# Norm tiles with the feature weight and the spread root in one DVE instruction, the shift on ACT, and both blocks of the first job by tile

## The chip, the cores and the metric

One core of one Trainium2 chip. The metric is device time in microseconds of one launch: 2413.69 us is the median of three runs of the kernel before (2411.8 to 2418.44).

## The reference, cut to what matters

A two-layer block over 512 latent tokens and 256 context tokens of width 1024. Layer 0 mixes with an SSD scan and a long convolution, layer 1 with windowed attention; each has a SwiGLU feed-forward. Ahead of each of these four projections every token vector is normed, weighted by feature and shifted by feature:

```
def rmsnorm(t, g):
    y = t * rsqrt(mean(t * t, axis=-1) + 1e-6)
    return y * g

h_l = rmsnorm(x, norm1_g[layer]) * (1.0 + mod_l[1]) + mod_l[0]      # latent tokens
h_c = rmsnorm(ctx, norm1_g[layer]) * (1.0 + mod_c[1]) + mod_c[0]    # context tokens
p = h @ w_in                                   # layer 0; layer 1: h @ w_qkv
...
h_l = rmsnorm(x, norm2_g[layer]) * (1.0 + mod_l[4]) + mod_l[3]      # before the feed-forward
gu = h_l @ ffn_w_in[layer]
```

So a normed element is x * root(token) * gain(feature, segment) + shift(feature, segment). The two segments are the latent and the context tokens.

## The kernel before

The activations lie with features on the partitions: a tensor is 8 tiles (`KT`) of 128 features by 768 tokens, and `SEGS` are its columns 0 to 511 (latent) and 512 to 767 (context). Layer 1's queries and its feed-forward use the latent columns alone.

Every product is made of three TensorE passes on rounded parts: a high part (rounded to fp32r) and a low part (the rest) for both weights and activations; high x high, high x low weight, low x high weight (L487, L488, L492). The weights' high part is a DVE copy (`split_high`, L1587) into `WH`, which has a single place for each of the two blocks of a job. The low part is a POOL subtraction (`low`, L2013), written over the weights. So the next job's block b can be split only when this job's block b is multiplied (`next_high` waits for `blocks_done`). Weights come in jobs of two 512 KB halves, into 3 slots, issued by SP (L431) when the job three places earlier is multiplied. In the first stage (`uv`) two of each three jobs are small ada jobs, so there the next large job's load is issued when the present one is multiplied.

A norm goes as follows. TensorE sums squares, ACT takes the root (L1178), DVE its reciprocal, and TensorE spreads it into PSUM as `NP` (L565). Then DVE, ACT, POOL and TensorE work tile by tile on 8 tiles: DVE makes the normed tile in `norm` with a multiplication of x by `NP` (L1576) and, after waiting for itself, one `tensor_scalar` per segment with gain and shift (L1578); ACT copies it into its high part (`high_parts`, L1184); POOL subtracts for the low part (`low_parts`, L2026). TensorE's first job after the norm (`two_blocks` with `by_tile`) waits per tile for the high part and then for the low part. It does so in block 0 alone: block 0 takes all 8 tiles, then block 1 takes the 8 tiles again, with no wait.

There are four such places: the `uv` stage (trace 178 to 217 us), layer 0's feed-forward (1104 to 1142 us), the q/k/v stage (1691 to 1728 us; 768 columns are normed, of which its first jobs multiply 512) and layer 1's feed-forward (2024 to 2043 us, 512 columns). In the q/k/v stage POOL issues the rope table's and the mask's loads (L2180, L2181) behind its last low part, and DVE waits for the rope table before it splits any weights of that stage. The final norm (L1573) has no such job behind it.

The key lines before:

```
TT(HN[:, k, lo:hi], X[:, k, lo:hi], NP[:, lo:hi], ALU.mult)              # L1576, DVE
TS(HN[:, k, a:b], HN[:, k, a:b], GA[...], MOD[...], ALU.mult, ALU.add)   # L1578, DVE, per segment
run(high[:, k, lo:hi], HN[:, k, lo:hi], ACT.Copy)                        # L1184, ACT
TT(HNL[:, k, lo:hi], HN[:, k, lo:hi], high[:, k, lo:hi], ALU.subtract)   # L2026, POOL
```

## Time and profile before

| | us |
|---|---|
| median of three runs | 2413.69 (2411.8 to 2418.44) |
| the profiled execution | 2418.78, of which 2417.0 is the span of its trace |
| TensorE busy | 2217.1 |
| DVE, POOL, ACT busy | 960.0, 856.9, 413.7 |
| mean granted TensorE clock | 0.933 |

The page gives busy time by engine, a picture of the span in 40 slices, and groups of instructions by line. The timeline gives single instructions: start, length, engine, line, what is written from what, and in brackets how long the engine was idle before it and who released it. TensorE's granted clock is told as a share: 1.00 is 2.4 GHz and 0.50 is 1.2 GHz. Several matmuls are in flight at once, so the distance between two starts is what one costs.

### The profile page before, as it was taken

The page shows a single profiled execution, that of the slowest core. Times are in us where ns is not written, and L with a number is a line of the kernel's source. Part 1 is how long each engine was busy: PE and PEld are TensorE (multiplying, and loading weights), DVE is VectorE, ACT ScalarE, POOL GpSimd, SP SyncE. Part 2 cuts the span into 40 slices and gives each one's busy share as a digit, 9 for nine tenths or more (in the row PEclk, how much of TensorE's full clock was granted, in tenths as well). Part 3 has the DMA queues.
Part 4 walks back from the last instruction along what each step waited for, and adds up shares of the span by engine and source line. Part 5 has one row for each costly group of instructions (what it writes and reads, how often), then busy time and mean ns, then how long its engine had stood idle before and what let it go on. Part 6 is the DMA issues. An engine that isn't in the chain of part 4 may idle for free. (4 is left out here: it accounts for less than half of the span.)

```text
span 2417.0 us, 30280 instructions
## 1 busy us (share of the span) xinstructions
PE 2217.1 (92%) x11978; PEld 1734.4 (72%) x11978; DVE 960.0 (40%) x1284; ACT 413.7 (17%) x769; POOL 856.9 (35%) x460
## 2 busy tenths in 40 slices
PE   7959998899998996997999999998787998999997
PEld 2436865688887774885888888887475666888886
DVE  3555354321234767335122112133525655322334
ACT  1211111001244553001000000000103631100110
POOL 0264353512223756323222332222421124444442
PEclk8777998999998997997999999999788998999998
DMA  8312432333311001110111221112110002223222
GB/s 302 135 52 96 152 111 101 107 113 126 102 44 53 1 2 43 56 67 26 61 61 48 74 71 61 53 60 70 61 45 18 1 28 69 95 78 112 91 82 73
DMA packets 50750, 181.52 MB, mean 75 GB/s; under 512 B 5815, under 2 KB 6071, under 8 KB 49688
## 3 DMA queue, kind: packets, MB, share of 16 engines
q1 hardware_dynamic: 48288, 163.60, 20.2%
q10 hardware_dynamic: 1848, 13.52, 1.5%
q0 software_dynamic: 512, 2.95, 0.3%
q8 instruction: 75, 1.23, 0.2%
q14 instruction: 27, 0.22, 0.0%
HBM read 177.95 MB, written 2.10 MB: 74 GB/s over the span
## 5 line engine op out<-in xcount | busy, mean ns | idle before, releaser
L2013 POOL TENSOR_TENSOR weights_lo<-weights,weights_hi 128x1024 fp32r<-128x1024 f32 (+1 forms) x232 | 514.4, 2218 | 1042.8 <-DVE weights_hi L1587 1042.8
L492 PE MATMUL psum<-normed_lo,weights_hi 128*128 128x512 f32 x1856 | 550.9, 360 | 12.0 <-POOL normed_lo L2026 11.9
L1587 DVE CAST weights_hi<-weights 128x1024 fp32r<-128x1024 f32 (+1 forms) x232 | 163.9, 707 | 921.1 <-PE psum L492 786.4
L487 PE MATMUL psum<-normed_hi,weights_hi 128*128 128x512 f32 (+1 forms) x1152 | 425.2, 369 | 16.1 <-ACT normed_hi L1184 16.1
L488 PE MATMUL psum<-normed_hi,weights_lo 128*128 128x512 f32 (+1 forms) x1152 | 404.8, 365 | 0.0
L492 PEld LDWEIGHTS psum<-normed_lo,weights_hi 128*128 128x128 f32 x1856 | 306.0, 193 | 43.7 <-POOL normed_lo L2026 26.3
L487 PEld LDWEIGHTS psum<-normed_hi,weights_hi 128*128 128x128 f32 x1152 | 221.6, 192 | 74.4 <-ACT normed_hi L1184 15.2
L487 PE MATMUL psum<-normed_first_hi,weights_hi 128*128 128x512 f32 x704 | 248.5, 353 | 16.1 <-POOL weights_lo L2013 9.3
L488 PEld LDWEIGHTS psum<-normed_hi,weights_lo 128*128 128x128 f32 x1152 | 222.7, 193 | 38.3 <-issue 1.5
L488 PE MATMUL psum<-normed_first_hi,weights_lo 128*128 128x512 f32 x704 | 226.7, 343 | 0.0
L487 PE MATMUL psum<-hidden_hi,weights_hi 128*128 128x512 f32 (+1 forms) x528 | 189.1, 358 | 0.0
L488 PE MATMUL psum<-hidden_hi,weights_lo 128*128 128x512 f32 (+1 forms) x528 | 178.9, 354 | 0.0
L487 PEld LDWEIGHTS psum<-normed_first_hi,weights_hi 128*128 128x128 f32 x704 | 135.8, 193 | 57.3 <-issue 10.8
L492 PE MATMUL psum<-hidden_lo,weights_hi 128*128 128x512 f32 (+1 forms) x528 | 160.4, 358 | 0.0
L488 PEld LDWEIGHTS psum<-normed_first_hi,weights_lo 128*128 128x128 f32 x704 | 136.3, 194 | 17.6 <-issue 1.2
L487 PEld LDWEIGHTS psum<-hidden_hi,weights_hi 128*128 128x128 f32 x528 | 99.1, 188 | 23.5
L488 PEld LDWEIGHTS psum<-hidden_hi,weights_lo 128*128 128x128 f32 x528 | 99.3, 188 | 15.0
L487 PE MATMUL psum<-mixed_hi,weights_hi 128*128 128x512 f32 (+1 forms) x256 | 90.5, 354 | 14.2 <-ACT mixed_hi L1373 8.0
L1618 DVE SCALAR_TENSOR_TENSOR temps<-psum,vectors,temps 128x511 f32<-128x511 f32 x112 | 63.8, 612 | 98.6 <-ACT temps L1198 97.6
L492 PEld LDWEIGHTS psum<-hidden_lo,weights_hi 128*128 128x128 f32 x528 | 87.1, 188 | 8.9
L1389 ACT ACTIVATE temps<-psum 128x768 f32<-128x768 f32 (+1 forms) x44 | 31.1, 707 | 355.7 <-PE psum L492 355.7
L1393 ACT ACTIVATE hidden_hi<-temps 128x768 f32 (+3 forms) x44 | 32.5, 740 | 342.9 <-DVE temps L1872 342.9
(281 smaller groups left out, 3015.1 us busy)
## 6 DMA issues: line engine op xcount, KB each, us to landing
weights<-in_wall SPq DMA_DIRECT2D x264, 512.0 KB, 4.0
weights<-in_wall SPq DMA_DIRECT2D x32, 384.0 KB, 3.2
weights<-in_wall SPq DMA_DIRECT2D x32, 320.0 KB, 3.0
residual<-in_xT ACTq DMA_DIRECT2D x2, 3072.0 KB, 10.4
phase<-in_tab ACTq DMA_DIRECT2D x3, 1280.0 KB, 7.0
out_T<-normed SPq DMA_DIRECT2D x2, 1024.0 KB, 4.3
normed<-in_window ACTq DMA_DIRECT2D x1, 1536.0 KB, 16.7
normed<-in_window POOLq DMA_DIRECT2D x1, 1536.0 KB, 7.7
```

The costliest lines, as they stand in the source:

```text
L487: mm(acc[:, lo:hi], WH[:, b, k, :], high[:, lo:hi], start=st, stop=False)
L488: mm(acc[:, lo:hi], WL[:, s, HALF * b + k, :], high[:, lo:hi], start=False, stop=False)
L492: ins = mm(acc[:, lo:hi], WH[:, b, k, :], low[:, lo:hi], start=False, stop=en)
L1389: run(T[:, 0, lo:hi], pair(0)[:, lo:hi], ACT.Silu).then_inc(pair_free[0], 1)
L1393: run(at_row(HIDH, r)[:, lo:hi], T[:, 1, lo:hi], ACT.Copy).then_inc(hid_hi, 1)
L1587: dve.tensor_copy(WH[:, b, 0:n, :], W[:, s, HALF * b:HALF * b + n, :]).then_inc(w_hi, 1)
L1618: ins = STT(t[:, a:e], p[:, a + shift:e + shift], w, t[:, a:e], ALU.mult, ALU.add)
L2013: TT(WL[:, s, at, :], W[:, s, at, :], WH[:, b, 0:width(gs[0], b), :].bitcast(f32), ALU.subtract).then_inc(w_lo, 1)
```

## The change

In `norm`, the two steps of DVE become one `scalar_tensor_tensor` per segment, (x * gain) * spread root, which reads x from SBUF and `NP` from PSUM. The shift moves to ACT: `high_parts` first runs one Identity activation per segment in place on the normed tile, with the shift as a per-partition bias, waits for itself, and then makes the high copy as before. A new function `both_by_tile` serves the first job of each of the four places: both blocks' weights and PSUM pairs are waited for at the start, then tiles 0 to 5 are multiplied for both blocks as they come, then tiles 6 and 7 for block 0, then tiles 6 and 7 for block 1.

```diff
--- before.py
+++ after.py
@@ -492,11 +492,42 @@
                         ins = mm(acc[:, lo:hi], WH[:, b, k, :], low[:, lo:hi], start=False, stop=en)
                 ins.then_inc(blocks_done, 1)
 
+            def both_by_tile(gs, i, rhs, segs, by_tile, after=None, last=True, together=6):
+
+
+                s = gs[0] % SLOTS
+                accs = []
+                for b in range(2):
+                    half_ready(gs, i, b)
+                    accs.append(pair(pair_ready(gs, i, b)))
+                order = [(k, (0, 1)) for k in range(together)] + [(k, (b,)) for b in range(2) for k in range(together, KT)]
+                for k, blocks in order:
+                    if blocks[0] == 0:
+                        by_tile[0](k)
+                    high, low = rhs(k)
+                    for b in blocks:
+                        for lo, hi in segs:
+                            mm(accs[b][:, lo:hi], WH[:, b, k, :], high[:, lo:hi], start=k == 0, stop=False)
+                            mm(accs[b][:, lo:hi], WL[:, s, HALF * b + k, :], high[:, lo:hi], start=False, stop=False)
+                    if blocks[0] == 0:
+                        by_tile[1](k)
+                    for b in blocks:
+                        for lo, hi in segs:
+                            ins = mm(accs[b][:, lo:hi], WH[:, b, k, :], low[:, lo:hi], start=False,
+                                     stop=last and k == KT - 1)
+                    if k == KT - 1:
+                        ins.then_inc(blocks_done, 1)
+                    if after:
+                        after(k, blocks)
+
             def two_blocks(gs, i, rhs, segs=SEGS, between=None, by_tile=None):
+                if by_tile:
+                    both_by_tile(gs, i, rhs, segs, by_tile)
+                    return
                 for b in range(2):
                     half_ready(gs, i, b)
                     u = pair_ready(gs, i, b)
-                    tiles(gs, pair(u), b, KT, rhs, segs, True, True, by_tile if b == 0 else None)
+                    tiles(gs, pair(u), b, KT, rhs, segs, True, True)
                     if b == 0 and between:
                         between()
 
@@ -1177,16 +1208,19 @@
                 n = 2 * segs[-1][1] // P
                 run(RS[0][:, 0:n], NS[:, 0:n], ACT.Sqrt, scale=1.0 / D, bias=vec("eps", 0)).then_inc(n_sqrt, 1)
 
-            def high_parts(muls, segs=SEGS, high=HNH):
+            def high_parts(muls, layer, shift, segs=SEGS, high=HNH):
                 lo, hi = segs[0][0], segs[-1][1]
                 for k in range(KT):
                     act.wait_ge(n_mul, muls + k + 1)
+                    for j, (a, b) in enumerate(segs):
+                        ins = run(HN[:, k, a:b], HN[:, k, a:b], Id, bias=MOD[:, layer, 8 * shift + k, j:j + 1])
+                    ch.link(ins)
                     run(high[:, k, lo:hi], HN[:, k, lo:hi], ACT.Copy).then_inc(hn_hi, 1)
 
 
             act.wait_ge(n_summed, 1)
             root()
-            high_parts(0, high=HNH0)
+            high_parts(0, 0, 0, high=HNH0)
 
             def conv_first(gs, i, b, wname, bname, blk, dst, wait=None):
 
@@ -1376,7 +1410,7 @@
                 sqrt_table()
                 act.wait_ge(n_summed, n + 1)
                 root(segs)
-                high_parts(KT * (n + 1), segs)
+                high_parts(KT * (n + 1), layer, 3, segs)
                 lo, hi = segs[0][0], segs[-1][1]
                 for half in range(2):
                     name = f"up{layer}{half}"
@@ -1399,7 +1433,7 @@
             sqrt_table()
             act.wait_ge(n_summed, 3)
             root()
-            high_parts(3 * KT)
+            high_parts(3 * KT, 1, 0)
 
             for n in range(5):
                 g = AT["qkv"] + n
@@ -1560,7 +1594,7 @@
                         ins = TT(even, even, odd, ALU.subtract)
                     ins.then_inc(kd_ev, 1)
 
-            def norm(n, which=None, layer=0, shift=0, segs=SEGS, last=False):
+            def norm(n, which=None, segs=SEGS, last=False):
 
                 lo, hi = segs[0][0], segs[-1][1]
                 dve.wait_ge(n_sqrt, n + 1)
@@ -1573,10 +1607,9 @@
                         STT(HN[:, k, lo:hi], X[:, k, lo:hi], vec("fin", k), NP[:, lo:hi], ALU.mult, ALU.mult) \
                             .then_inc(fin_ready, 1)
                         continue
-                    ch.link(TT(HN[:, k, lo:hi], X[:, k, lo:hi], NP[:, lo:hi], ALU.mult))
                     for j, (a, b) in enumerate(segs):
-                        ins = TS(HN[:, k, a:b], HN[:, k, a:b], GA[:, which, k, j:j + 1],
-                                 MOD[:, layer, 8 * shift + k, j:j + 1], ALU.mult, ALU.add)
+                        ins = STT(HN[:, k, a:b], X[:, k, a:b], GA[:, which, k, j:j + 1], NP[:, a:b],
+                                  ALU.mult, ALU.mult)
                     ins.then_inc(n_mul, 1)
 
 
@@ -1605,7 +1638,7 @@
             ins.then_inc(mods_a, 1)
             dve.wait_ge(mods_a, 1)
             ch.link(gains(0, 0, 1, "n1"))
-            norm(0, 0, 0, 0)
+            norm(0, 0)
 
             def conv(gs, i, b, wname, n, blk, count, dst=None):
 
@@ -1858,7 +1891,7 @@
                     dve.memset(MARK[:, 0:1], 0.0).then_inc(sums_ready, 1)
 
             def feed_forward(layer, n, segs):
-                norm(n + 1, 2 * layer + 1, layer, 3, segs)
+                norm(n + 1, 2 * layer + 1, segs)
                 lo, hi = segs[0][0], segs[-1][1]
                 for half in range(2):
                     name = f"{layer}{half}"
@@ -1882,7 +1915,7 @@
             dve.wait_ge(x_in, 32)
             res("out0", 0, 2, SEGS)
             feed_forward(0, 1, SEGS)
-            norm(3, 2, 1, 0)
+            norm(3, 2)
 
 
             dve.wait_ge(rope_in, 16)
```

## Rows read from the trace of the kernel before

**Rows 1.** The page's first part: busy time of TensorE, share, instructions.
```profile
PE 2217.1 (92%) x11978; PEld 1734.4 (72%) x11978; DVE 960.0 (40%) x1284; ACT 413.7 (17%) x769; POOL 856.9 (35%) x460
```

**Rows 2.** Timeline, first normed tiles: start us, length us, engine, line, operation, [idle before].
```profile
178.39 0.95 DVE L1576 TENSOR_TENSOR normed<-residual,psum 128x768 f32<-128x768 f32 x1 [3.02 <-PE psum L565]
...
181.15 2.48 DVE L1578 TENSOR_SCALAR normed<-normed,gains,mods 128x512 f32<-128x512 f32 x2
...
181.20 1.82 POOL L2026 TENSOR_TENSOR normed_lo<-normed,normed_first_hi 128x768 fp32r<-128x768 f32 x1 [4.01 <-ACT normed_first_hi L1184]
...
181.27 0.47 PE L487 MATMUL psum<-normed_first_hi,weights_hi 128*128 128x512 f32 x1 [2.92 <-ACT normed_first_hi L1184]
```

**Rows 3.** Line L1844 (one PSUM, one SBUF input): count, minimum/median/maximum ns.
```profile
L1844 DVE SCALAR_TENSOR_TENSOR residual<-psum,mods,residual x72: 468/744/751, 973.3 to 2400.7; 128x512 f32 x30, 128x512 f32<-128x512 f32 x18, 128x256 f32 x18, 128x256 f32<-128x256 f32 x6
```

**Rows 4.** Groups of ACT by shape, SBUF to SBUF: busy us, mean ns.
```profile
L1184 ACT ACTIVATE normed_hi<-normed 128x768 fp32r<-128x768 f32 x16 | 13.5, 843 | 45.8 <-DVE normed L1578 45.8
...
L1393 ACT ACTIVATE hidden_hi<-temps 128x512 f32 x18 | 11.4, 632 | 114.6 <-DVE temps L1872 114.6
...
L1274 ACT ACTIVATE phase<-phase,vectors 128x768 f32<-128x768 f32 x8 | 7.5, 931 | 0.0
```

**Rows 5.** Timeline of ACT, eight copies with no wait between them.
```profile
903.51 5.98 ACT L1362 ACTIVATE mixed_hi<-phase 128x768 fp32r<-128x768 f32 x8
```

**Rows 6.** Timeline from block 1 of the first job to the next job's start.
```profile
207.51 0.63 PE L487 MATMUL psum<-normed_first_hi,weights_hi 128*128 128x512 f32 x1
...
207.75 0.99 ACT L1198 ACTIVATE temps<-psum,vectors 128x768 f32<-128x768 f32 x1 [2.99 <-PE psum L492]
...
209.43 0.56 PE L487 MATMUL psum<-normed_first_hi,weights_hi 128*128 128x512 f32 x1
...
212.14 0.69 DVE L1587 CAST weights_hi<-weights 128x1024 fp32r<-128x1024 f32 x1 [1.06 <-DMA weights<-in_wall]
...
212.92 2.40 POOL L2013 TENSOR_TENSOR weights_lo<-weights,weights_hi 128x1024 fp32r<-128x1024 f32 x1 [6.27 <-DVE weights_hi L1587]
...
217.01 1.92 PE L523 MATMUL psum<-weights,phase 128*32 128x512 f32 x16
...
218.87 0.50 PE L487 MATMUL psum<-normed_first_hi,weights_hi 128*128 128x512 f32 x1
```

**Rows 7.** The same of layer 0's feed-forward: block 1 starts, refill, block 1 ends.
```profile
1133.15 0.63 PE L487 MATMUL psum<-normed_hi,weights_hi 128*128 128x512 f32 x1
...
1134.17 2.40 POOL L2013 TENSOR_TENSOR weights_lo<-weights,weights_hi 128x1024 fp32r<-128x1024 f32 x1 [1.88 <-DVE weights_hi L1587]
...
1142.52 0.69 DVE L1587 CAST weights_hi<-weights 128x1024 fp32r<-128x1024 f32 x1 [8.43 <-PE psum L492]
```

**Rows 8.** The same of the q/k/v stage, with the rope table's load.
```profile
1694.37 0.77 PE L487 MATMUL psum<-normed_hi,weights_hi 128*128 128x512 f32 x1 [2.92 <-ACT normed_hi L1184]
...
1719.67 0.58 POOL L2180 DMA_DIRECT2D phase<-in_rope  x1
...
1723.61 0.69 DVE L1587 CAST weights_hi<-weights 128x1024 fp32r<-128x1024 f32 x1 [6.66 <-DMA phase<-in_rope]
...
1728.39 0.69 DVE L1587 CAST weights_hi<-weights 128x1024 fp32r<-128x1024 f32 x1 [4.08 <-PE psum L492]
```

**Rows 9.** The same of layer 1's feed-forward, 512 columns.
```profile
2025.92 0.77 PE L487 MATMUL psum<-normed_hi,weights_hi 128*128 128x512 f32 x1 [2.11 <-ACT normed_hi L1184]
...
2037.61 0.40 PE L487 MATMUL psum<-normed_hi,weights_hi 128*128 128x512 f32 x1
...
2043.38 0.69 DVE L1587 CAST weights_hi<-weights 128x1024 fp32r<-128x1024 f32 x1 [4.88 <-PE psum L492]
```

**Rows 10.** Stretches: length, TensorE busy us (count), granted clock, DMA share, GB/s.
```profile
182.40:206.70 24.30, 18.59 (x42) 0.50 0.08 20
...
2025.90:2032.40 6.50, 6.11 (x13) 0.50 0.00 0
...
1750.20:1756.00 5.80, 3.67 (x7) 0.71 0.28 90
```

## The prediction

> **What bounds the kernel now.** I read the page's first part, then the timeline at the four places that the change touches. TensorE is busy 92% of the span [rows 1], so the time falls only where TensorE waits or runs at its low clock, and outside the four places nothing is touched. At the first place the reader is to see a relay. DVE's multiplication starts at 178.39, TensorE's first matmul at 181.27 and block 1 of the same job at 207.51 [rows 2, 6]. Block 0 thus takes 26.24 us for 8 tiles, 3.28 us a tile, while its matmuls cost far less: at the full clock block 1 shows 7 tiles in 7.58 us (209.43 to 217.01) [rows 6], the first of them partly slow, and layer 1's feed-forward shows 8 tiles of 512 columns in 5.53 us (2037.61 to the cast at 2043.38, less the 0.24 us from matmul to cast seen at 207.51 and 207.75) [rows 6, 9]: 0.69 for 512 columns, so 1.04 for 768. I take 1.05 and 0.70. Nor is DVE's own work 3.28 us. Its `tensor_scalar` pair starts at 181.15 and needs 2.48 us, and POOL's subtraction starts at 181.20 and ends at 183.02 [rows 2]: the first of the pair waits for POOL. So in the normed tiles DVE bounds, held up by POOL, and TensorE waits at 0.50 of its clock, which is its 1.2 GHz level [rows 10].
>
> **Part 1: DVE.** Removed per tile: a 768-column multiplication (0.95 us), a wait on itself, and the pair of 2.48 us [rows 2]. Added: two `scalar_tensor_tensor` with one input in PSUM. The residual additions have this form: median 744 and at most 751 ns at 512 columns, 468 at 256, over 72 that ran beside POOL's work as well as without it, so POOL never held one up [rows 3]. I take 0.74 + 0.47 = 1.2 us a tile. DVE no longer waits for anybody and is done with 8 tiles after some 10 us.
>
> The Trainium skill (SBUF — State Buffer, Who interferes with whom) says that DVE and GpSimd share a pair of ports that one instruction holds for its whole length, and that a DVE instruction with at most one SBUF input, outside the two-port modes, does not contend. It would make the `tensor_scalar` the culprit and the new form free. The trace agrees: 2.48 us beside POOL's 1.82 us [rows 2], 751 ns at most for the other form [rows 3].
>
> **Part 2: ACT.** Before, one copy: 843 ns at 768 columns, 632 at 512 [rows 4]; that is 0.21 us per 256 columns, so some 421 ns at 256. Added per tile: two Identity activations with a vector operand, and a wait of ACT for itself. An activation with one vector operand took 931 against 843 ns, 88 more [rows 4]. So 0.72 + 0.51 us, less the overlap of neighbours: eight copies took 5.98 us, not 6.74, 0.11 each [rows 5]. ACT's wait for itself is not shown; the nearest row is a handover between engines, DVE's cast (end 212.83) to POOL (212.92), 0.09 us [rows 6]. Inside one engine I take 0.05, with 0.2 as the dear end; below 0 it cannot go, since it only orders two instructions. Period of ACT: 0.72 + 0.51 - 0.11 + 0.05 + 0.84 - 0.08 = **1.93 us** for 768 columns, and 0.72 + 0.05 + 0.63 - 0.08 = 1.32 us for 512; without overlaps and with the dear wait 2.3 and 1.55. POOL needs 1.82 and some 0.07 for the handover, which hides behind ACT. The first tile comes at 178.39 + 1.15 (DVE) + 1.12 + 0.05 + 0.84 (ACT) + 0.14 (two handovers) = 181.69 instead of 181.27 [rows 2]: **0.42 us** later.
>
> **Part 3: both blocks by tile.** Per tile TensorE now has 2 x 1.05 = 2.1 us of work against ACT's 1.93, so it bounds and hides ACT and POOL. Sixteen tile-blocks cost 16.8 us at the full clock. To this comes 0.5 us in the first tile: the high passes of both blocks last 1.4 us, the low part comes after 1.9. And the clock is low at first: in the relay it was 0.50 throughout [rows 10], and once TensorE no longer waited (207.51) it reached full pace by 209.43, where a tile then took 1.08 instead of 1.92 us [rows 6]. I take 5 us at the low level, which costs 2.5 us; the ends are 1.9 us as at 207.51 (costs 1.0) and 7 us (costs 3.5), since from 2025.90 to 2032.40 TensorE was busy 6.11 of 6.50 us and still at 0.50 [rows 10].
>
> What is late next is the refill of the weights. The next job's block 0 can be split only when block 0 is done. Before, block 1 hid this: 8 tiles. Now only tiles 6 and 7 of block 1 do, 2.1 us.
>
> *Place 1 (uv).* Before: block 1 begins at 207.51, ACT reads block 0 at 207.75, the next weights must still be loaded (the cast waits for their DMA until 212.14), and POOL's low part ends at 215.32 [rows 6]. The refill takes 7.9 us. After: TensorE starts at 181.27 + 0.42 = 181.7, ends block 1 at 181.7 + 16.8 + 0.5 + 2.5 = 201.5 and block 0 at 199.4. The next large job starts at 199.4 + 7.9 = 207.3; the ada job between them covers only 1.9 of it (217.01 to 218.87) [rows 6], so TensorE stands some 3.9 us. Before, it started at 218.87: 11.6 us earlier. A wait is followed by low clock: 1750.20 to 1756.00 holds a wait of some 2 us (3.67 busy of 5.80) and a mean clock of 0.71 [rows 10], so 0.58 x 5.80 = 3.4 us at the low level, which cost 1.7. I charge 1.8 us (0 to 2.5). **Gain 9.8** (7.8 to 12.9). The SP queue holds the loads behind `blocks_done` in the same order as before, and POOL's product and DVE's convolution stand ahead of block 1's refill, which has the next block 0 (8.4 us) as cover.
>
> *Place 2 (layer 0's feed-forward).* The loads are here long since. The refill is 1133.15 to POOL's end at 1136.57, 3.5 us with the handover [rows 7]. The relay was as long as at place 1, so it began at 1106.9; now 1107.3. End of block 1 at 1107.3 + 19.8 = 1127.1, of block 0 at 1125.0, next job at 1128.5, a wait of 1.4 us. Before: 1142.52 - 0.24 = 1142.3. 13.8 us, less 0.8 for the clock (0 to 1.8): **gain 13.0** (11.1 to 15.2).
>
> *Place 3 (q/k/v).* Norm of 768 columns, matmuls of 512: 1.4 us a tile, so ACT bounds with 1.93. Start 1694.37 + 0.42 = 1694.8, last high part 13.5 later, last low part at 1710.2. Then POOL issues the rope load, and DVE's next cast waits for it, 3.94 us from issue (1719.67 to 1723.61) [rows 8]: 1714.2. Cast and low part take 3.3: TensorE's next job at 1717.5, though it was done with the first at 1711.9. Before: 1728.39 - 0.24 = 1728.15. 10.6 us, less 1.8 for the clock: **gain 8.8** (7.4 to 10.6; a later tile of ACT, up to 0.37 us each, would take 2.6 more).
>
> *Place 4 (layer 1's feed-forward).* The relay is short here: blocks 0 and 1 together take 2025.92 to 2043.1 [rows 9]. After: 2026.1 + 16 x 0.70 + 0.3 + 2.5 = 2040.1, block 0 at 2038.7, refill 3.5, next job at 2042.2. 0.9 us, less 1.2 for the clock: **-0.3** (-1.9 to 2.3).
>
> **The sum.** 9.8 + 13.0 + 8.8 - 0.3 = 31.3 us (24.4 to 41.0, all bounds one way). The profiled execution took 2418.78 us, its span 2417.0; the median is 2413.69. Its span would become 2385.7 and its time 2387.5. That execution lies 5.1 us above the median, spread over 2417 us, so the gain carries over whole: 2413.69 - 31.3 = **2382.4 us**.
>
> **The rivals.** *A, the clock stays low in the joint jobs.* The condition is that small gaps between the groups of two accumulations keep the clock at 0.50. A tile-block is then 1.92 us (207.51 to 209.43) [rows 6], 1.28 for 512 columns. Place 1: block 1 ends at 212.4, block 0 at 208.6, next job 216.5, 2.4 less 1.0 for the clock; place 2: 1138.0, 4.3; place 3 stays with the rope load at 8.8; place 4: 2026.1 + 20.5 = 2046.6, 3.5 lost. Together 11.0: **2402.7 us**. For it: at 0.50 TensorE was busy 18.59 of 24.30 us and did not rise [rows 10]. Against it: here the work never runs out. Chance 8%.
>
> The Trainium skill (TensorE: Matmul & The Clock Gate, A second HAM failure mode: psum-queue depth-cycling) tells of a kernel that cycled through PSUM banks, stood briefly between its groups and so lost its clock again and again. That is rival A, as the joint job changes its PSUM pair twice a tile; by the forecast that rule does not bite. No row here shows two accumulations in turn.
>
> *B, the new DVE form waits for POOL after all.* A tile then takes 1.82 + 1.2 + 0.05 = 3.07 us, 2.1 at 512 columns. Place 1's next job starts at 213.5 (3.6 gained with the clock), place 2's at 1134.7 (6.8), place 3's at 1725.4 (1.0), place 4 loses 3.5: 7.9, **2405.8 us**. 751 ns at most speaks against it [rows 3]. Chance 4%.
>
> *C, slower: ACT becomes the relay's bound.* The mechanism is what ACT must do between Identity and Copy, a reload of its function tables above all; its place is the 32 normed tiles. With x us more per tile, the next jobs start at 205.5, 1126.7, 1717.5 and 2040.5, each plus 8x. Against the starts before, that gives 13.4 + 15.6 + 10.6 + 2.6 - 32x, less some 5.6 for the clock, so it decides from x = 1.1 us. At x = 2.5 it costs 43 us: **2457 us**. Against it: at 207.75 ACT ran an Identity right behind the root and the copies with nothing in front but its wait for TensorE [rows 6]. Chance 3%.
>
> *D, part of the gain is given back later*, where place 1's head start meets the next loads, since each large job there waits for a load that is issued when the one before ends. The next block's refill of 7.9 us has 8.4 + 1.9 us of cover, a margin of 2.4 us only. If all of place 1 is lost: **2392 us**. Chance 6%.
>
> *E, no low clock anywhere*, neither at the start nor behind the new waits: all upper bounds, some 41 us, **2373 us**. Chance 7%.
>
> **How the numbers follow.** The forecast, 2382.4 with 2373 to 2389 from the bounds, has 72%; A 8, B 4, C 3, D 6, E 7%. The range for 8 in 10 goes to D, E and A, as the clock is the least certain term: 2371 to 2403. A measurement of this kernel tells 0.3%, 7.2 us, from no change. Faster by more: 0.94. Within it: 0.03 (B or C in part). Slower by more: 0.03 (C).
>
> **What would show it.** In the trace after: DVE's new line at 0.74 and 0.47 us also beside POOL's subtraction; ACT's period at 1.9 us with no table load inside; first-job matmuls gapless from the second tile on, block 1's end near 201.5, 1127, 1712 and 2040; then waits of some 3.9, 1.4, 5.5 and 2 us, ended by POOL's low weights, with a low clock behind the longer ones. Wrong would be: tiles of 1.9 us in TensorE to the end (A), DVE idle or stretched beside POOL (B), ACT above 3 us a tile (C), and later `uv` jobs that wait more than before (D).

## The result and the profile after

The changed kernel took 2382.35 us (median of four runs, 2380.05 to 2386.81), the kernel before 2414.68 us beside it (2411.8 to 2418.44): a ratio of 0.9859, 95% interval 0.9842 to 0.9875. The profiled execution of after took 2386.81 us with a span of 2385.0; forecast were 2387.5 and 2385.7.

The page's first part of the kernel after, columns as in [rows 1]:

```profile
PE 2192.0 (92%) x11978; PEld 1731.1 (73%) x11978; DVE 905.8 (38%) x1252; ACT 443.5 (19%) x825; POOL 856.4 (36%) x460
```

TensorE runs the same 11978 matmuls and is busy 25.1 us less. At the low clock a matmul of 512 columns is busy 0.63 us (207.51 in [rows 6]) and at the full clock 0.39 (188.16 below), so this is relay time that is gone. DVE loses 54.2 us, ACT gains 29.8, POOL is as before.

The timeline of the kernel after at place 1, to be read against [rows 2, 6]:

```profile
179.03 8.49 DVE L1611 SCALAR_TENSOR_TENSOR normed<-residual,gains,psum 128x512 f32<-128x512 f32 x16 [3.02 <-PE psum L596]
180.20 1.12 ACT L1216 ACTIVATE normed<-normed,mods 128x512 f32<-128x512 f32 x2 [4.53 <-DVE normed L1611]
...
182.28 15.09 POOL L2059 TENSOR_TENSOR normed_lo<-normed,normed_first_hi 128x768 fp32r<-128x768 f32 x8 [4.46 <-ACT normed_first_hi L1218]
182.34 0.47 PE L510 MATMUL psum<-normed_first_hi,weights_hi 128*128 128x512 f32 x1 [3.35 <-ACT normed_first_hi L1218]
...
188.16 0.39 PE L510 MATMUL psum<-normed_first_hi,weights_hi 128*128 128x512 f32 x1
...
190.26 0.39 PE L510 MATMUL psum<-normed_first_hi,weights_hi 128*128 128x512 f32 x1
...
198.68 0.39 PE L510 MATMUL psum<-normed_first_hi,weights_hi 128*128 128x512 f32 x1
198.88 0.99 ACT L1232 ACTIVATE temps<-psum,vectors 128x768 f32<-128x768 f32 x1 [3.44 <-PE psum L516]
...
202.90 0.69 DVE L1620 CAST weights_hi<-weights 128x1024 fp32r<-128x1024 f32 x1 [0.68 <-PE psum L554]
203.67 2.34 POOL L2046 TENSOR_TENSOR weights_lo<-weights,weights_hi 128x1024 fp32r<-128x1024 f32 x1 [6.31 <-DVE weights_hi L1620]
206.07 0.50 PE L487 MATMUL psum<-normed_first_hi,weights_hi 128*128 128x512 f32 x1 [3.28 <-POOL weights_lo L2046]
```

The reader is to see four things. DVE makes all 16 segments in 8.49 us without a stop. POOL's eight subtractions start 1.89 us apart (15.09 us in all), the distance at which ACT makes the tiles without a pause, so the relay runs at ACT's pace; POOL is close behind, its subtractions last 1.84 to 1.86 us each. TensorE goes from tile to tile in 2.10 us (188.16 to 190.26), both blocks together (from here on the joint job), and has block 0 done at 198.68. Then it stands 3.28 us, until POOL has the low part of the next weights: the relay has made room for a new wait.

The waits of TensorE at the four places of the kernel after (line, released by: us in total, times, longest), by windows 150 to 260, 1075 to 1150, 1645 to 1730 and 1975 to 2060 us:

```profile
PE psum L487 <- POOL weights_lo L2046: 3.3, 1, 3.3
...
PE psum L487 <- POOL weights_lo L2046: 1.2, 1, 1.2
...
PE psum L487 <- POOL weights_lo L2046: 5.7, 1, 5.7
PE psum L516 <- POOL normed_lo L2059: 2.0, 4, 0.9
...
PE psum L487 <- POOL weights_lo L2046: 1.9, 1, 1.9
```

And what TensorE's clock did (stretch: length, busy us of PE, PEld, DVE, ACT, POOL, clock, DMA share, GB/s): from the first matmul of place 1 for 3.76 us, the rest of the joint job, and 3.5 us behind the new waits of places 1 to 4.

```profile
182.34:186.10 3.76, 3.76 (x13) 3.23 (x14) 3.76 (x8) 3.70 (x7) 3.66 (x3) 0.56 0.00 0
186.10:198.50 12.40, 12.40 (x72) 10.85 (x71) 1.42 (x3) 9.18 (x15) 11.08 (x6) 1.00 0.24 82
...
206.07:209.57 3.50, 3.50 (x13) 3.03 (x14) 1.84 (x1) 0.00 (x0) 2.87 (x2) 0.59 0.97 303
1117.49:1120.99 3.50, 3.50 (x20) 3.07 (x21) 2.59 (x3) 0.85 (x1) 2.41 (x1) 1.00 0.42 147
1692.73:1696.23 3.50, 3.50 (x8) 2.81 (x9) 0.00 (x0) 0.00 (x0) 2.28 (x1) 0.50 0.06 23
2008.92:2012.42 3.50, 3.50 (x8) 2.80 (x9) 2.72 (x3) 0.63 (x1) 2.37 (x1) 0.51 0.41 142
```

To place the gain I cut both traces at DVE's reciprocal that heads each norm, which stands at 175.14, 1100.75, 1688.23, 2021.47 and (final norm) 2404.5 us before, and at 175.78, 1091.21, 1663.51, 1988.38 and 2372.51 after. A stretch from one to the next holds one place and what follows it. "At the next job" is the gain in the time from the reciprocal to the first matmul of the next large job.

| place | at the next job: forecast | measured | given back after it: forecast | measured | gain: forecast | measured |
|---|---|---|---|---|---|---|
| 1, uv | 11.6 | 13.4 | 1.8 | 3.3 | 9.8 | 10.2 |
| 2, layer 0's feed-forward | 13.8 | 15.3 | 0.8 | 0.1 | 13.0 | 15.2 |
| 3, q/k/v | 10.6 | 10.7 | 1.8 | 2.3 | 8.8 | 8.4 |
| 4, layer 1's feed-forward | 0.9 | 1.1 | 1.2 | 2.2 | -0.3 | -1.1 |
| sum | 36.9 | 40.5 | 5.6 | 7.9 | 31.3 | 32.6 |

The first reciprocal came 0.64 us later after than before; that leaves 32.0, the difference of the spans.

### The profile page after: what moved, and what is told of

Read it like the earlier page. It is cut to its first block, busy times and chain, and to the rows that moved or that the text cites. A ratio compares the mean times of both kernels' runs of the same rounds, so it can differ in the third digit from the quotient of the medians.

```text
span 2385.0 us, 30305 instructions
## 1 busy us (share of the span) xinstructions
PE 2192.0 (92%) x11978; PEld 1731.1 (73%) x11978; DVE 905.8 (38%) x1252; ACT 443.5 (19%) x825; POOL 856.4 (36%) x460
## 4 chain that ended last, share of the span: by engine, by line
PE 83%; DVE 6%; POOL 6%; DMA 2%; ACT 1%; issue 1%; ACTq 0%; DVEq 0%; SPq 0%
PE psum L487 20%; PE psum L492 20%; PE psum L488 20%; PE psum L1068 2%; PE psum L1056 2%; PE psum L1085 2%; PE psum L554 1%; POOL weights_lo L2046 1%; PE psum L708 1%; DMA weights<-in_wall 1%; PE psum L893 1%; PE psum L918 1%; PE psum L676 1%; DVE normed L1793 1%; PE psum L638 1%
## 5 line engine op out<-in xcount | busy, mean ns | idle before, releaser
L492 PE MATMUL psum<-normed_lo,weights_hi 128*128 128x512 f32 x1760 | 511.9, 354 | 0.0
L487 PE MATMUL psum<-normed_hi,weights_hi 128*128 128x512 f32 x1088 | 394.5, 363 | 8.8 <-POOL weights_lo L2046 8.8
L488 PE MATMUL psum<-normed_hi,weights_lo 128*128 128x512 f32 x1088 | 376.8, 361 | 0.0
L492 PEld LDWEIGHTS psum<-normed_lo,weights_hi 128*128 128x128 f32 x1760 | 287.7, 191 | 16.9
L487 PEld LDWEIGHTS psum<-normed_hi,weights_hi 128*128 128x128 f32 x1088 | 206.6, 190 | 57.7 <-POOL weights_lo L2046 6.4
L487 PE MATMUL psum<-normed_first_hi,weights_hi 128*128 128x512 f32 (+1 forms) x672 | 235.6, 351 | 11.8 <-POOL weights_lo L2046 11.3
L488 PEld LDWEIGHTS psum<-normed_hi,weights_lo 128*128 128x128 f32 x1088 | 207.7, 191 | 35.3 <-issue 1.0
L488 PE MATMUL psum<-normed_first_hi,weights_lo 128*128 128x512 f32 (+1 forms) x672 | 215.8, 342 | 0.0
L487 PEld LDWEIGHTS psum<-normed_first_hi,weights_hi 128*128 128x128 f32 x672 | 129.3, 192 | 48.1 <-POOL weights_lo L2046 13.2
L488 PEld LDWEIGHTS psum<-normed_first_hi,weights_lo 128*128 128x128 f32 x672 | 129.6, 193 | 16.6 <-issue 1.2
L487 PE MATMUL psum<-mixed_hi,weights_hi 128*128 128x512 f32 (+1 forms) x256 | 91.5, 357 | 14.2 <-ACT mixed_hi L1407 8.0
L1427 ACT ACTIVATE hidden_hi<-temps 128x768 f32 (+3 forms) x44 | 32.6, 740 | 334.2 <-DVE temps L1905 334.2
## 6 DMA issues: line engine op xcount, KB each, us to landing
residual<-in_xT ACTq DMA_DIRECT2D x2, 3072.0 KB, 10.6
```

What stands on the lines that cost most here:

```text
L487: mm(acc[:, lo:hi], WH[:, b, k, :], high[:, lo:hi], start=st, stop=False)
L488: mm(acc[:, lo:hi], WL[:, s, HALF * b + k, :], high[:, lo:hi], start=False, stop=False)
L492: ins = mm(acc[:, lo:hi], WH[:, b, k, :], low[:, lo:hi], start=False, stop=en)
L1427: run(at_row(HIDH, r)[:, lo:hi], T[:, 1, lo:hi], ACT.Copy).then_inc(hid_hi, 1)
```

## The experiments

Theory 1 is the account of the prediction: the old pace of 3.3 us a tile came from DVE being held up by POOL, the new form ends that, and the joint multiplication trades an earlier end of block 1 for a wait on the refill. Its rivals are told in each expectation. All runs of a batch stand beside the kernel before on the same chip (medians there 2416.01, 2416.41 and 2417.25 us), and ratios are to it.

**Each half of the change alone.** First the new norm without the joint job:

```diff
-                if by_tile:
-                    both_by_tile(gs, i, rhs, segs, by_tile)
-                    return
...
-                    tiles(gs, pair(u), b, KT, rhs, segs, True, True)
+                    tiles(gs, pair(u), b, KT, rhs, segs, True, True, by_tile if b == 0 else None)
```

> The changed kernel with both blocks of the first job taken one after the other again, block 0 by tile, block 1 behind it; the norm's new split between DVE and ACT stays. Theory 1 (the relay's pace is what paid, and the joint job gives most of its own gain back as a wait for the weights' refill): block 0 then ends with the last low part, near 197.5 us at place 1, block 1 hides the refill. Next jobs some 9.8 us (place 1), 9.5 (place 2), 10.7 (place 3) earlier and 0.9 later (place 4) than in the kernel before: 2414 - 29 = 2385 us, within 3 us of the full change, with no wait for low weights behind the first jobs. Theory 2 (the joint job is worth what it takes from block 1, 6.3 us at each 768-column place and more of the gain with it): 2400 us or more.

Measured: 2383.56 us, ratio 0.9866 (0.9852 to 0.988). Then the joint job with the old norm:

```diff
-                        ins = STT(HN[:, k, a:b], X[:, k, a:b], GA[:, which, k, j:j + 1], NP[:, a:b],
-                                  ALU.mult, ALU.mult)
+                    ch.link(TT(HN[:, k, lo:hi], X[:, k, lo:hi], NP[:, lo:hi], ALU.mult))
+                        ins = TS(HN[:, k, a:b], HN[:, k, a:b], GA[:, which, k, j:j + 1],
+                                 MOD[:, layer, 8 * shift + k, j:j + 1], ALU.mult, ALU.add)
```

> The kernel before with the joint multiplication alone; DVE's norm in three instructions with gain and shift, ACT's copy only. Theory 1: the relay still comes at 3.37 us a tile and bounds; the joint job ends some 7 us sooner at places 1 and 2 but the refill then stands open, 7.4 and 3.5 us behind block 0. Gains 2, 5, -0.5 and -0.5: 2414 - 6 = 2408 us. Theory 2 (the joint job carries the gain): 2395 us or less.

Measured: 2410.04 us, ratio 0.9971 (0.9962 to 0.9979). In the same batch the changed kernel itself ran once more:

> The changed kernel itself, as the measure for the other three on the same chip: 2382 us, 31 to 33 us below the kernel before, by either theory.

Measured: 2378.84 us, ratio 0.9851 (0.9832 to 0.9869). So the new norm alone brings 32.5 of the 37.2 us of this batch, the joint job alone 6.0. On top of the new norm the joint job adds 4.7 us by the medians, but the two intervals overlap, so that is not shown to be different from none. A single profile can't decide it either: up to the first norm's reciprocal all kernels of this study run the same code, and yet it stands between 169.93 us (two tiles together) and 177.15 (shift left out). The stretches say where it would be: 576.40 us with the norm alone against 571.33 with both, at place 2, and 914.09 against 913.69 at place 1. Place 1 shows why. Timeline of the kernel with the norm alone, from block 1's first matmul to the next large job:

```profile
195.70 0.39 PE L487 MATMUL psum<-normed_first_hi,weights_hi 128*128 128x512 f32 x1
...
200.47 0.69 DVE L1617 CAST weights_hi<-weights 128x1024 fp32r<-128x1024 f32 x1 [1.22 <-DMA weights<-in_wall]
...
201.24 2.41 POOL L2043 TENSOR_TENSOR weights_lo<-weights,weights_hi 128x1024 fp32r<-128x1024 f32 x1 [6.05 <-DVE weights_hi L1617]
...
206.02 0.50 PE L487 MATMUL psum<-normed_first_hi,weights_hi 128*128 128x512 f32 x1
```

Block 0 is done at 195.7, the refill ends at 203.65 under block 1's eight tiles, and the next job starts at 206.02 with no wait. The joint job takes this cover away and pays with the 3.3 us above and a low clock behind them.

In the kernel with the old norm and the joint job DVE's old pair is still there, and so is its pace:

```profile
182.68 2.51 DVE L1609 TENSOR_SCALAR normed<-normed,gains,mods 128x512 f32<-128x512 f32 x2
...
186.09 2.50 DVE L1609 TENSOR_SCALAR normed<-normed,gains,mods 128x512 f32<-128x512 f32 x2
```

A tile takes 3.41 us (182.68 to 186.09), and TensorE waits for ACT's high part tile after tile.

**How many tiles together.** The number of tiles multiplied for both blocks goes from 6 to 4, then to 2. With fewer, block 0 ends earlier and more of block 1 covers the refill.

```diff
-            def both_by_tile(gs, i, rhs, segs, by_tile, after=None, last=True, together=6):
+            def both_by_tile(gs, i, rhs, segs, by_tile, after=None, last=True, together=4):
```

> The changed kernel with tiles 0 to 3 for both blocks together and tiles 4 to 7 for each block alone (6 and 2 in the changed kernel). Block 0 then ends as soon as the last low part allows, about 1 us sooner than with 6, and block 1's tail of four tiles covers 4.2 instead of 2.1 us of the refill. Theory 1 (the refill behind block 0 is the new bound, so the time follows block 0's end, not block 1's): 1 us less at places 1, 2 and 4 and a shorter wait with less low clock: 2 to 4 us below the full change. Theory 3 (only block 1's end counts): no change.

Measured: 2373.62 us, ratio 0.9827 (0.9814 to 0.984).

> Tiles 0 and 1 for both blocks, tiles 2 to 7 for each block alone. Theory 1: block 0 cannot end sooner than with 4 (it waits for the last low part), while block 1's tail is now 6.3 us, longer than the 3.5 us refill of places 2 and 4 and near the uncovered rest at place 1. TensorE waits for tiles again meanwhile. Place 1 as with 4, places 2 to 4 some 1 to 2 us later than with 4: 2376 us, between the changed kernel and the one with 4. Theory 3 (only block 1's end counts): 2386 us.

Measured (second batch): 2375.32 us, ratio 0.9828 (0.9812 to 0.9844). The wait at place 1 shrinks from 3.28 us to 1.39 with four tiles:

```profile
201.17 2.36 POOL L2046 TENSOR_TENSOR weights_lo<-weights,weights_hi 128x1024 fp32r<-128x1024 f32 x1 [5.69 <-DVE weights_hi L1620]
...
203.58 0.50 PE L487 MATMUL psum<-normed_first_hi,weights_hi 128*128 128x512 f32 x1 [1.39 <-POOL weights_lo L2046]
```

The kernel with four is the fastest by median: 42.4 us below the kernel before. It is 5.2 us below the changed kernel by the medians of one batch, though the intervals still touch, and its profile doesn't show that the number of tiles did all of it. Its stretch 3 is 6.4 to 7.1 us shorter (318.48 against 324.87 us in the changed kernel and 325.58 in its repetition). The wait for the refill there is 2.1 us against 5.7 and 5.5, but the next job starts only 0.8 and 0.5 us sooner behind the reciprocal (28.47 us against 29.22 and 28.95), as the joint job ends later when four tiles of block 1 are left to the end. Another 2.6 and 1.8 us come from less low clock behind the shorter wait: the next job's first 36 matmuls take 13.17 us against 15.72 and 14.99. The rest, 3.0 and 4.8 us, lies in the q/k/v stage that follows, whose code is the same, and comes from the clock told of below. With two tiles together that part took 65.64 us, with four 62.66, in the changed kernel 65.68 and 67.42.

**Is it POOL that held DVE up?** If that alone made the pace, a `tensor_scalar` put ahead of each tile of the new form should bring the old pace back.

```diff
                     for k in range(KT):
+                    TS(Tt[:, 384 * k:384 * k + 384], X[:, k, 0:384], 1.0, None, ALU.mult)
                     for j, (a, b) in enumerate(segs):
```

> The changed kernel with one more DVE instruction ahead of each normed tile: a tensor_scalar of 384 columns from SBUF to SBUF, into unused scratch. It needs about 0.47 us, so DVE's own work is 1.06 + 0.47 = 1.53 us a tile, below ACT's 1.9 and TensorE's 2.1. Theory 1 (the old pace of 3.37 us came from DVE's tensor_scalar and POOL's subtraction standing in each other's way): both again wait for each other; POOL then needs 1.84 + 0.47 us a tile, above TensorE's 2.1, and at place 4 1.8 against 1.4. Starts 0.5 later at four places, then 2, 2, 3 and 3 us: about 10 us slower than the changed kernel. Theory 4 (the count and length of DVE's instructions is what cost): only the later starts, 2 us, as in the twin run with tensor_tensor.

Measured: 2380.23 us, ratio 0.9845 (0.9828 to 0.9862). The expected 10 us didn't come; a miss. Beside it the same place with a `tensor_tensor` of one SBUF and one PSUM input:

> The twin of the run before: the additional instruction is a tensor_tensor of the same 384 columns, x from SBUF by the spread root from PSUM, into the same scratch, about 0.54 us. Theory 1: it never meets POOL, DVE stays below ACT's pace, and only the four starts are 0.54 us later: 2 us slower than the changed kernel, POOL's subtraction at 1.82 us as before. Theory 4: the same as its twin or slightly more.

Measured: 2384.1 us, ratio 0.9861 (0.9841 to 0.9882). The twin that doesn't meet POOL (547 to 565 ns over 32) is not faster than the one that does; it is 3.9 us slower by the medians, with overlapping intervals. The timeline of the kernel with the added `tensor_scalar` (L1610) at place 1:

```profile
180.21 0.36 DVE L1610 TENSOR_SCALAR temps<-residual 128x384 f32<-128x384 f32 x1
180.48 1.13 DVE L1612 SCALAR_TENSOR_TENSOR normed<-residual,gains,psum 128x512 f32<-128x512 f32 x2
181.09 9.54 POOL L2060 TENSOR_TENSOR normed_lo<-normed,normed_first_hi 128x768 fp32r<-128x768 f32 x5 [4.73 <-ACT normed_first_hi L1218]
181.53 1.61 DVE L1610 TENSOR_SCALAR temps<-residual 128x384 f32<-128x384 f32 x1
...
184.11 0.94 DVE L1610 TENSOR_SCALAR temps<-residual 128x384 f32<-128x384 f32 x1
```

Ahead of POOL's first subtraction the instruction takes 0.36 us; the first one that starts inside it (181.53) takes 1.61 and ends 0.1 us behind the subtraction (181.09 + 9.54/5 = 183.0); the later ones take 0.94 to 0.97. The hold is there, but POOL's pace isn't touched: 9.54 us for five, 1.91 each. DVE passes one held instruction per POOL instruction, so it still makes a tile in 1.91 us (184.11 to 186.02), and it had two tiles ready and a third under way when POOL began. At place 1 of this kernel ACT waits for DVE once, for the first tile.

So here a hold cost nothing that the runs could show, as DVE had a lead. In the old form DVE had none, and no pause either: its multiplication and its pair fill the tile. The pair lasts 0.87 us for tile 0, before POOL begins, and 2.48 us for tile 1 and the later ones. With 0.94 + 0.87 = 1.8 us a tile (an estimate from these rows) DVE's own work wouldn't have set a pace of 3.38 us. Its pair of tile 1 and POOL's subtraction of tile 0 come together (181.15 and 181.20 [rows 2]), and the two wait for each other in turn, as the first pair, the held segment alone and the next turn of the kernel before show:

```profile
179.38 0.87 DVE L1578 TENSOR_SCALAR normed<-normed,gains,mods 128x512 f32<-128x512 f32 x2
...
181.15 2.15 DVE L1578 TENSOR_SCALAR normed<-normed,gains,mods 128x512 f32<-128x512 f32 x1
...
183.66 0.84 ACT L1184 ACTIVATE normed_first_hi<-normed 128x768 fp32r<-128x768 f32 x1 [2.54 <-DVE normed L1578]
...
184.52 2.48 DVE L1578 TENSOR_SCALAR normed<-normed,gains,mods 128x512 f32<-128x512 f32 x2
...
184.58 1.81 POOL L2026 TENSOR_TENSOR normed_lo<-normed,normed_first_hi 128x768 fp32r<-128x768 f32 x1 [1.56 <-ACT normed_first_hi L1184]
```

POOL's 1.82 us (181.20 to 183.02), 0.61 for the rest of DVE's pair (to 183.63), 0.87 for ACT's copy with its handover (to 184.50) and 0.08 to POOL's next start make the old period of 3.38 us. This is read from the trace; no run takes the hold alone out of the old norm.

**The lead taken away.** To see what the pace is worth when DVE has no lead, DVE may begin tile k only when ACT has rounded tile k-1.

```diff
                     for k in range(KT):
+                    if k:
+                        dve.wait_ge(hn_hi, KT * shifted[0] + k)
                     for j, (a, b) in enumerate(segs):
```

> VectorE may begin tile k of a norm only when ScalarE has rounded tile k-1; nothing else differs from the changed kernel. This takes VectorE's lead away. The chain of one tile is then 1.2 us (VectorE) + 1.1 us (Identity) + 0.84 us (Copy) + some 0.1 us of hand-over = 3.2 us at 768 columns, against 1.89 us in the changed kernel; over seven tiles some 9 us at places 1 and 3, some 4 us at places 2 and 4 (512 columns, about 2.0 against 1.35 us). All theories: about 2405 us. It is the base of the next two.

Measured (third batch): 2408.83 us, ratio 0.9973 (0.9957 to 0.999). A tile takes 3.21 us (177.79 to 181.00). So nearly the whole gain hangs on the pace of the relay: this kernel keeps the new instructions and the joint job, and stands where the old norm with the joint job stands (ratio 0.9971). Then the extra instruction behind that wait, in both forms:

> As the one before, with a tensor_tensor of 384 columns out of PSUM ahead of each tile, behind the wait, so that it stands in the chain (0.55 us in the run with a lead). All theories: 28 tiles by 0.55 us = 15 us more than the one before, about 2420 us.

Measured: 2426.44 us, ratio 1.0048 (1.0033 to 1.0063), 17.6 us above the wait alone where 15 were expected.

> As the one before, with the tensor_scalar from SBUF to SBUF in place of the tensor_tensor, in the chain as well. It comes free just when GpSimd begins the low part of tile k-1. Theory 1 (this form waits until GpSimd's instruction ends, and only VectorE's lead hid that in the run with a lead): 1.85 + 0.35 us per tile at 768 columns and 1.25 + 0.35 at 512, seven tiles each, four places: some 50 us above the first, about 2455 us, and 35 us slower than the one with the tensor_tensor; the instruction lasts some 2 us in the trace. Theory 6 (the wait for GpSimd is small and the old pace had another cause): 28 by 0.35 us = 10 us above the first, about 2415 us, and 5 us faster than the one with the tensor_tensor.

Measured: 2420.94 us, ratio 1.0018 (1.0008 to 1.0028). Theory 1 expected 2455 and is missed by 34 us; theory 6 had 2415. The trace says why. Timeline of the kernel with the `tensor_scalar` (L1615) behind the wait:

```profile
178.35 0.36 DVE L1615 TENSOR_SCALAR temps<-residual 128x384 f32<-128x384 f32 x1 [2.06 <-ACT normed_first_hi L1218]
178.40 2.01 POOL L2065 TENSOR_TENSOR normed_lo<-normed,normed_first_hi 128x768 fp32r<-128x768 f32 x1 [4.71 <-ACT normed_first_hi L1218]
```

The same stretch of the kernel with the wait alone:

```profile
177.79 1.14 DVE L1616 SCALAR_TENSOR_TENSOR normed<-residual,gains,psum 128x512 f32<-128x512 f32 x2 [2.06 <-ACT normed_first_hi L1218]
177.84 1.83 POOL L2064 TENSOR_TENSOR normed_lo<-normed,normed_first_hi 128x768 fp32r<-128x768 f32 x1 [4.46 <-ACT normed_first_hi L1218]
```

Both engines are released by the same ACT copy, and DVE starts 0.05 us before POOL. None of the 32 `tensor_scalar` is held (0.36 us each); it is POOL's subtraction that grows, from 1.83 to 2.01 us. A tile takes 3.47 us, 0.26 more than with the wait alone. So the two still get in each other's way, but this time DVE goes first, and theory 1's price didn't fall due. Theory 6's number is near, yet its reason (the wait for POOL is small) is contradicted by the 2.15 and 1.61 us above. The test with a held instruction inside the chain was thus not made, and no run here prices the hold on the path by itself. What stays open is who goes first when both start together: in the kernel before DVE's segment is 0.05 us ahead in the trace too (181.15 and 181.20) and is held for 2.15 us. It has 512 columns instead of 384, two vector operands, and follows straight behind another DVE instruction, where here DVE was idle; no run tells which of these decides.

The Trainium skill (SBUF — State Buffer, Who interferes with whom) says that when a DVE instruction in a two-port mode meets a GpSimd one, the one that issues first has the shared ports for its whole instruction and the other is blocked fully. That one of the two is held agrees with the rows; by the starts in the trace alone the rule doesn't tell which, as DVE is 0.05 us ahead in both cases and lost one. And POOL's 0.18 us is less than the 0.31 us (178.40 to 178.71) for which a full block would have kept it out.

**What the shift costs on ACT.** Identity is left out, so the norm's shift is missing from the output.

```diff
-                    for j, (a, b) in enumerate(segs):
-                        ins = run(HN[:, k, a:b], HN[:, k, a:b], Id, bias=MOD[:, layer, 8 * shift + k, j:j + 1])
-                    ch.link(ins)
```

> ScalarE's Identity with the bias is left out, so the norm's shift is missing from the result; VectorE's new form and the joint multiplication stay. It prices what the moved shift costs on ScalarE. Theory 1 (ScalarE's pace of 1.89 us lies below TensorE's 2.10, so that only the head of each of the four norms is on the path): TensorE begins 1.1 us earlier at each place at 768 columns and 0.8 us at 512, some 4 us below the changed kernel. Theory 3 (ScalarE is a bound all along): 8 tiles by some 0.5 us more at each place, 10 us or more below it.

Measured: 2375.05 us, ratio 0.9824 (0.9802 to 0.9846): 3.8 us below the changed kernel's 2378.84, of another batch, with overlapping intervals. In the trace the first matmul comes 2.16 us behind DVE's first tile (180.40 to 182.56) instead of 3.31, which by four places is the expected 4 us. Had ACT been the bound all along, 10 us or more were expected. Outside place 3, where its pace does bound (see below), it isn't.

**A version to shorten that start.** Four tiles together, and ACT writes the high part first, straight from the unshifted tile with the bias, and then shifts in place for POOL.

```diff
                     for j, (a, b) in enumerate(segs):
+                        ins = run(high[:, k, a:b], HN[:, k, a:b], Id, bias=MOD[:, layer, 8 * shift + k, j:j + 1])
+                    ins.then_inc(hn_hi, 1)
+                    for j, (a, b) in enumerate(segs):
                         ins = run(HN[:, k, a:b], HN[:, k, a:b], Id, bias=MOD[:, layer, 8 * shift + k, j:j + 1])
-                    ch.link(ins)
-                    run(high[:, k, lo:hi], HN[:, k, lo:hi], ACT.Copy).then_inc(hn_hi, 1)
+                    ins.then_inc(a_ch, 1)
```

> With 4 tiles together, and ACT's order turned: first Identity with the shift from the normed tile straight into the high part (per segment), which is reported at once, then the same in place for POOL's subtraction. Four short activations a tile instead of two and a copy: 4 instructions, 2 x (0.72 + 0.51) less 4 x 0.11 = 2.0 us, just below TensorE's 2.1. The first high part comes 0.85 us sooner at each place. Theory 1 (TensorE bounds the joint part, starts sooner and never waits for ACT): 2 to 3 us below the kernel with 4 together, 2371 us. Theory 5 (ACT at 2.0 to 2.1 becomes the relay's bound, worst at place 3 where TensorE needs 1.4): no gain or 1 to 2 us lost.

Measured: 2377.22 us, ratio 0.9832 (0.9817 to 0.9847). No gain over the order with the copy. Timeline, the late tiles of place 1:

```profile
188.91 0.62 PE L516 MATMUL psum<-normed_lo,weights_hi 128*128 128x512 f32 x2 [0.66 <-POOL normed_lo L2065]
...
190.94 0.62 PE L516 MATMUL psum<-normed_lo,weights_hi 128*128 128x512 f32 x2 [0.71 <-POOL normed_lo L2065]
```

Two segments with a bias twice cost ACT 2.03 us a tile (188.91 to 190.94) against 1.89, and in the last four tiles, where TensorE needs only 1.05 each, that pace is the bound.

## Why the prediction was right, point by point

**Part 1, DVE.** 0.74 + 0.47 = 1.2 us a tile was forecast. Line L1611 shows 475/742/748 ns (least, median, most) over 56, of which 35 ran beside a POOL instruction; a tile takes 1.06 us, since neighbours overlap. Its independence of POOL, taken from [rows 3], held. What the prediction said of the old kernel is right in the traces, but it lacked the second half: where DVE has a lead, a hold need not be a bound. The forecast didn't need it, as it was made from the new form's own durations.

**Part 2, ACT.** 1.93 us a tile forecast, 1.89 measured (POOL's eight in 15.09 us). Identity at 512 columns took 709 ns in the mean (forecast 720), at 256 494 (510). The first matmul stands 3.31 us behind DVE's first tile (179.03 to 182.34), against 178.39 to 181.69 = 3.30 forecast.

**Part 3, the joint job.** TensorE's 2.10 us per tile came as forecast. From the first matmul to block 0's end 17.7 us were forecast (181.7 to 199.4) and 16.34 measured. The low clock is the term that was too dear: 3.76 us at a mean of 0.56 is (1 - 0.56)/0.5 x 3.76 = 3.3 us at the low level, which cost 1.65 us, not 2.5. The 0.5 us for the first tile didn't show either. The refill took 7.4 us (198.68 to 206.07) for 7.9.

**The waits.** Forecast 3.9, 1.4, 5.5 and 2 us; measured 3.28, 1.21, 5.73 and 1.91, all ended by POOL's low weights as named. This is the step that made the forecast near: without it the sum would have been 12 us too good.

**Place 3** went by the step named for it. ACT's pace bounds there: TensorE waits 0.23 to 0.90 us for POOL's low parts, and then DVE's cast waits for the rope table:

```profile
1684.99 0.58 POOL L2213 DMA_DIRECT2D phase<-in_rope  x1
1685.11 0.50 PE L516 MATMUL psum<-normed_lo,weights_hi 128*128 128x512 f32 x1 [0.90 <-POOL normed_lo L2059]
...
1689.18 1.29 DVE L1620 CAST weights_hi<-weights 128x1024 fp32r<-128x1024 f32 x2 [13.93 <-DMA phase<-in_rope]
1689.96 5.04 POOL L2046 TENSOR_TENSOR weights_lo<-weights,weights_hi 128x1024 fp32r<-128x1024 f32 x2 [3.87 <-DVE weights_hi L1620]
1692.73 0.79 PE L487 MATMUL psum<-normed_hi,weights_hi 128*128 128x512 f32 x1 [5.73 <-POOL weights_lo L2046]
```

The load took 4.2 us from its issue to the cast, 3.94 before [rows 8].

**The size that was off** is the low clock behind a wait. It was charged with 1.8 + 0.8 + 1.8 + 1.2 = 5.6 us. With the start of the same matmul taken in both traces, from the next job's first one until the distance stays the same, after needs 4.80 us for before's 3.24 at place 1, 3.97 for 3.86 at place 2, 15.72 for 11.58 at place 3 and 3.51 for 1.85 at place 4. That is 1.6 + 0.1 + 4.1 + 1.7 = 7.5 us. Place 3 was charged with less than half of what it cost; the clock was low from the first matmul to 1698.33 and again from 1705.15 to 1708.56, behind the first of the stage's own gaps. At place 2, where the wait is only 1.21 us, it stayed at 1.00. The term isn't steady either: in the repeated run of the same kernel it is 1.5 + 0.1 + 3.4 + 0.1 = 5.1 us, with no low clock at place 4.

The column "given back" of the table holds more than this. At place 1 another 1.6 us stand in one short stretch of low clock at 619.7 us, more than 400 us behind the norm (the same matmuls take 63.10 us for 61.55), and the repeated run hasn't got it (61.54). At place 3 the q/k/v stage gave 1.8 us back by a higher mean clock (65.68 for 67.48), and at place 4 0.6 us stand at the final norm.

The error of +3.6 us at the next jobs and of -2.3 us behind them go against each other, so the sum is nearer than its terms. That the median was met within 0.1 us is luck: four executions of the changed kernel lie 6.8 us apart, and beside the next batch's kernel before the gain was 37.2 us, where 31.3 were forecast.

**The rivals.** A (clock low to the end of the joint job) fell: 1.00 from 186.10 to 198.50, though the job changes its PSUM pair twice a tile. The rule of the Trainium skill (TensorE: Matmul & The Clock Gate, A second HAM failure mode: psum-queue depth-cycling), which speaks of short pauses between the groups, thus did not bite: in that stretch TensorE was busy 12.40 of 12.40 us. B fell with L1611's 748 ns. C fell: no table load, and 3.31 us to the start. D, the head start given back at the next loads, fell as well: TensorE's waits for low weights between 222 and 975 us are 14.2 us in four, 15.5 before, and the lead over the kernel before is 11.2 us at 210.87 and 11.3 at 339.78. E fell with the clocks above.

## What to carry to other kernels

A stretched instruction in a trace need not be a bound: where the engine that suffered it had a lead over those that wait for it, stretches of 0.94 to 1.61 us cost nothing that could be measured. Ask first whether it stands in the chain, and when in the other engine's instruction it arrives. When a relay between engines is sped up, look for the refill that the slow relay hid, and price it before the gain. And consider leaving as much of the later block behind as the refill is long, because a joint multiplication that ends both blocks at once has no cover left: four and two tiles together had the lower medians here than six, though with overlapping intervals.

## What the runs showed of the hardware that was not expected

**The clock moves a stage by several us with the same gaps in it.** The q/k/v stage has four gaps of 2.20 us in TensorE, the same in the kernel before, in the changed one and with four tiles together. Windows of 90 us from its first full job on, columns as above; first the repeated run of the changed kernel, then the one with four tiles together:

```profile
1685.10:1775.10 90.00, 77.74 (x339) 61.02 (x340) 21.40 (x32) 5.21 (x8) 21.74 (x10) 0.88 0.15 50
```

```profile
1685.30:1775.30 90.00, 78.00 (x398) 63.37 (x399) 21.75 (x33) 5.21 (x8) 21.48 (x9) 0.96 0.16 51
```

Both do the same work with the same gaps, but at 0.96 the gaps lie 15.35 us apart (1695.53 to 1710.88) and at 0.88 they lie 16.91 us apart (1695.96 to 1712.87), as the low level sets in behind the gaps or doesn't. Before had 0.92. Between the same two matmuls of the stage this makes 67.42 us against 62.66, some 5 us with nothing changed in the stage's code, which is as much as the joint job is worth by the medians. The changed kernel's two profiles differ as well (65.68 and 67.42). What decides where the low level sets in stays open; effects of this size need more than one profile.

**Two refills too close together get in each other's way.** At places 2 and 4, where the two blocks end 2.1 and 1.4 us apart, the cast for block 1 meets POOL's low part of block 0. It takes 1.59 us at place 2 (1116.32). Timeline of place 4:

```profile
2005.66 0.69 DVE L1620 CAST weights_hi<-weights 128x1024 fp32r<-128x1024 f32 x1 [9.56 <-PE psum L516]
2006.43 2.35 POOL L2046 TENSOR_TENSOR weights_lo<-weights,weights_hi 128x1024 fp32r<-128x1024 f32 x1 [3.20 <-DVE weights_hi L1620]
2007.05 2.29 DVE L1620 CAST weights_hi<-weights 128x1024 fp32r<-128x1024 f32 x1 [0.69 <-PE psum L516]
```

2.29 us instead of 0.69, ending 0.56 us behind POOL's end. It costs nothing here, since block 0 of the next job covers it, but it looks like the hold of the old norm: DVE's instruction ends soon behind POOL's.
